# Heads normed and rotated by groups of product columns inside the tile loop

## What is computed

```python
def rms_norm(x, g):
    y = xf * lax.rsqrt(jnp.mean(xf * xf, axis=-1, keepdims=True) + EPS)
    return (y * g).astype(x.dtype)

def partial_rope(x, cos, sin):
    x1, x2, rest = xf[..., :half], xf[..., half:ROT_DIM], xf[..., ROT_DIM:]
    return jnp.concatenate([x1 * cos - x2 * sin, x2 * cos + x1 * sin, rest], axis=-1)

def qk_prep(t, g, cos, sin):
    return partial_rope(rms_norm(t, g), cos, sin)
...
hn = rms_norm(h, norm_mix[layer])
q, k, v = jnp.split(h @ w_in, ODD_SPLITS, axis=-1)
q = qk_prep(q.reshape(B, S, SWA_Q_HEADS, HEAD_DIM), qn, cos, sin)
k = qk_prep(k.reshape(B, S, SWA_KV_HEADS, HEAD_DIM), kn, cos, sin)
```

## Time and profile before

| | us |
|---|---|
| median of 3 runs | 2880.73 (2880.12 to 2882.5) |
| the profiled execution | 2879.53 |
| its span, first to last instruction | 2877.8 |
| TensorE busy | 2601.2 (90%) |
| VectorE busy | 1753.1 (61%) |
| ScalarE busy | 1206.5 (42%) |
| GpSimd busy | 632.8 (22%) |
| mean granted TensorE clock | 0.953 of 2.4 GHz |
| "qk" matmuls, first to last start | 392.5 to 655.9 |
| "all" matmuls, first to last start | 1597.6 to 1849.0 |

### The profile page before, as it was taken

One profiled execution on the slowest core, in us unless ns is written; L12 is line 12 of the kernel. 1 busy time (PEld: TensorE's weight loads), 2 busy tenths in 40 slices (PEclk: granted clock), 3 DMA queues, 4 the chain that ended last, 5 costly groups with the idle time before them and its releaser, 6 DMA issues. The chain is left out here.

```text
span 2877.8 us, 50000 instructions
## 1 busy us (share of the span) xinstructions
PE 2601.2 (90%) x14981; PEld 2201.3 (76%) x14984; DVE 1753.1 (61%) x3200; ACT 1206.5 (42%) x2278; POOL 632.8 (22%) x800
## 2 busy tenths in 40 slices
PE   6999989996979967999996899699979986999997
PEld 5999978885858866888885787578858875888786
DVE  4222245555767658776774777678843338777875
ACT  3222121114871114666764322188831114666764
POOL 3100003221110002333332233311100002434443
PEclk9999999998989978999998899899989987999999
DMA  7232223334446625776884455342235423988995
GB/s 278 99 106 105 86 87 119 102 114 160 152 146 236 233 92 210 292 290 246 303 336 186 173 173 179 118 155 88 69 112 204 175 88 131 309 292 255 343 317 133
DMA packets 171817, 524.61 MB, mean 182 GB/s; under 512 B 50232, under 2 KB 78016, under 8 KB 142656
## 3 DMA queue, kind: packets, MB, share of 16 engines
q1 hardware_dynamic: 138688, 441.27, 42.7%
q0 software_dynamic: 33024, 82.04, 9.9%
HBM read 399.14 MB, written 157.61 MB: 193 GB/s over the span
## 5 line engine op out<-in xcount | busy, mean ns | idle before, releaser
L1850 PE MATMUL ps<-moe_parts,moe_xT 128*128 (+1 forms) x2232 | 541.3, 399 | 14.0 <-issue 13.9
L1850 PEld LDWEIGHTS ps<-moe_parts,moe_xT 128*128 128x128 f32 x2232 | 417.4, 190 | 102.7 <-issue 16.3
L1989 DVE TENSOR_TENSOR moe_parts<-expert_w,moe_parts 128x1024 fp32r<-128x1024 f32 x384 | 449.8, 1219 | 33.5 <-ACT moe_parts L1930 27.0
L643 PE MATMUL ps<-in_gate_w,in_gate_hnT 128*128 128x384 f32 (+1 forms) x1536 | 318.4, 366 | 7.8 <-POOLq L614 7.8
L643 PEld LDWEIGHTS ps<-in_gate_w,in_gate_hnT 128*128 128x128 f32 x1536 | 277.9, 189 | 37.7 <-issue 7.8
L1255 PE MATMUL ps<-out_w,out_catT 128*128 128x512 f32 x1260 | 295.2, 393 | 2.5 <-ACT out_catT L1308 2.4
L1930 ACT ACTIVATE moe_parts<-expert_w 128x1024 fp32r<-128x1024 f32 x256 | 263.3, 1056 | 69.0 <-issue 46.5
L1850 PE MATMUL ps<-moe_parts,moe_hidT 128*128 (+1 forms) x1116 | 281.0, 401 | 2.6 <-ACT out_w L1951 2.6
L1255 PEld LDWEIGHTS ps<-out_w,out_catT 128*128 128x128 f32 x1260 | 234.4, 188 | 51.7 <-issue 3.2
L643 PE MATMUL ps<-in_qk_w,in_qk_hnT 128*128 128x512 f32 x1152 | 263.8, 392 | 10.1 <-DMA in_qk_hnT<-hnT_d 10.1
L643 PEld LDWEIGHTS ps<-in_qk_w,in_qk_hnT 128*128 128x128 f32 x1152 | 217.9, 189 | 55.7 <-issue 10.2
(11 more groups left out here) (257 smaller groups left out, 4051.8 us busy)
## 6 DMA issues: line engine op xcount, KB each, us to landing
expert_w<-in_w_gate SPq DMA_DIRECT2D x64, 1024.0 KB, 8.5
expert_w<-in_w_up SPq DMA_DIRECT2D x64, 1024.0 KB, 10.9
expert_w<-in_w_down SPq DMA_DIRECT2D x64, 1024.0 KB, 6.4
hnT_d<-in_gate_hnT SPq DMA_DIRECT2D x16, 1024.0 KB, 6.0
in_qk_hnT<-hnT_d SPq DMA_DIRECT2D x16, 1024.0 KB, 6.4
hn_d<-out_hn SPq DMA_DIRECT2D x32, 512.0 KB, 2.6
out_w<-y_d SPq DMA_DIRECT2D x32, 512.0 KB, 6.1
in_gate_xt<-in_x SPq DMA_DIRECT2D x16, 512.0 KB, 4.2
```

What stands on the lines that cost most here:

```text
L643: last = nc.tensor.matmul(bank(gi), hnT[:, s.slot(2), a, k, :], w[:, b, k, c0:c0 + wd], start=(a + b + k == 0), stop=((a, b) == terms_of[- ...
L1850: last = nc.tensor.matmul(out, left[:, a, k, :], right(b, k), start=(a + b + k == 0), stop=(a == 1 and k == K_ - 1))
L1989: nc.vector.tensor_tensor(parts[:, j, 1, at], K.expert_w[:, j, at], parts[:, j, 0, at].bitcast(F32), ALU.subtract).then_inc(done, 1)
```

## The change

In `project_in`, q and k heads of every tile are now squared, normed and rotated group by group, in the loop. `square_heads(s, part)` waits only for the group's own copy; `rms_heads` and `norm_rotate` run once per group, with counts `s.n * G + part + 1`. VectorE's step becomes: squares(s-1, group 2), rest(s-1, group 1), norm(s+1), rest(s-1, group 2), squares(s, 0), turn_out(s+1), rest(s, 0), squares(s, 1), add_terms(s+2). GpSimd's: `rms_tile(s+1)`, then the heads of (s-1, 2), (s, 0), (s, 1). `roped` still comes after the last group of a tile. The same elements are computed, in three times as many instructions. Behind the loop, only group 2's squares and the rests of groups 1 and 2 of the last tile are left.

```diff
--- before.py
+++ after.py
@@ -592,7 +592,7 @@
                 rms(own_, rx[:, j:j + 1], rx[:, j:j + 1], D, rms_x)
 
             def rms_heads(s, part=0, h0=0, h1=NQK):
-                alone(g, sum_q, s.n + part + 1, K.tick)
+                alone(g, sum_q, s.n * G + part + 1, K.tick)
                 rms(own_, rq[:, h0:h1], ssq[:, h0:h1], HD, rms_q)
 
             def step(s):
@@ -603,8 +603,11 @@
                 if gating:
                     alone(g, sum_v, s.n + 1, K.tick)
                     rms(own_, rv[:, :], ssv[:, :], SGU, rms_v)
-                elif not isinstance(s.n, int) or s.n >= 1:
-                    rms_heads(s.plus(-1))
+                else:
+                    if not isinstance(s.n, int) or s.n >= 1:
+                        rms_heads(s.plus(-1), G - 1, *by_group[G - 1])
+                    for part in range(G - 1):
+                        rms_heads(s, part, *by_group[part])
             rms_tile(Step(0, 0, 2))
             if gating:
 
@@ -612,10 +615,9 @@
                 own_.link(g.affine_select(out=ws[:, :, :], in_=ws[:, :, :], compare_op=ALU.is_ge, fill=0.0,
                                           base=0, pattern=[[0, SG], [1, P]], channel_multiplier=-1))
                 g.sem_inc(power_set, 1)
-            looped(g, NT, 2, 2, step, own_, 1 if kept else 3, head=1)
+            looped(g, NT, 2, 2, step, own_, 3 if gating else G if kept else G + 2, head=1)
             if qk_too:
-                for part, (h0, h1) in enumerate(by_group):
-                    rms_heads(Step(NT // 2 - 1, 1, 2), part, h0, h1)
+                rms_heads(Step(NT // 2 - 1, 1, 2), G - 1, *by_group[G - 1])
 
         @block.tensor
         def _(pe):
@@ -708,17 +710,19 @@
                 nc.vector.tensor_tensor(hnT[:, j, 1, :, :], tp.rearrange("p (k c) -> p k c", k=DK),
                                         hnT[:, j, 0, :, :].bitcast(F32), ALU.subtract).then_inc(x_low.sem, 1)
 
-            def square_heads(s, groups_out=G, h0=0, h1=NQK):
-                until(v_, act_out, s.n * G + groups_out)
+            def square_heads(s, part):
+                h0, h1 = by_group[part]
+                until(v_, act_out, s.n * G + part + 1)
                 at = slice(h0 * HD, h1 * HD)
                 qk = qk_[:, s.slot(nb), at]
                 own_.link(nc.vector.tensor_tensor(sq[:, at], qk, qk, ALU.mult))
                 nc.vector.tensor_reduce(ssq[:, h0:h1], sq[:, at].rearrange("p (h c) -> p h c", c=HD), AX, ALU.add).then_inc(sum_q.sem, 1)
 
-            def norm_rotate(s, part=0, h0=0, h1=NQK, last=True):
+            def norm_rotate(s, part):
+                h0, h1 = by_group[part]
                 n = h1 - h0
                 heads = qk_[:, s.slot(nb), h0 * HD:h1 * HD].rearrange("p (h c) -> p h c", c=HD)
-                until(v_, rms_q, s.n + part + 1)
+                until(v_, rms_q, s.n * G + part + 1)
                 own_.link(nc.vector.tensor_tensor(heads, heads, rq[:, h0:h1].unsqueeze(2).broadcast_to([P, n, HD]), ALU.mult))
                 parts = [(i, lo, hi) for i, lo, hi in ((0, h0, min(h1, NQ)), (1, max(h0, NQ), h1)) if lo < hi]
                 for i, lo, hi in parts:
@@ -738,7 +742,7 @@
                 own_.link(nc.vector.tensor_tensor(rot[:, 3, 0:n, :], x1, sin, ALU.mult))
                 own_.mark(nc.vector.tensor_tensor(x1, rot[:, 0, 0:n, :], rot[:, 1, 0:n, :], ALU.subtract))
                 own_.link(nc.vector.tensor_tensor(x2, rot[:, 2, 0:n, :], rot[:, 3, 0:n, :], ALU.add))
-                if last:
+                if part == G - 1:
                     v_.sem_inc(roped.sem, 1)
 
             def v_norm(s):
@@ -760,17 +764,23 @@
             def step(s):
                 heads_too = qk_too and (not isinstance(s.n, int) or s.n >= 1)
                 if heads_too:
-                    square_heads(s.plus(-1))
+                    square_heads(s.plus(-1), G - 1)
+                    norm_rotate(s.plus(-1), G - 2)
                 if s.plus(1).within(NT) and not (gating and isinstance(s.n, int) and s.n == 0):
                     norm(s.plus(1))
                 if gating:
                     v_norm(s)
                 if heads_too:
-                    norm_rotate(s.plus(-1))
+                    norm_rotate(s.plus(-1), G - 1)
+                if qk_too:
+                    square_heads(s, 0)
                 if s.plus(1).within(NT):
                     turn_out(s.plus(1))
                 if gating:
                     gate(s)
+                if qk_too:
+                    norm_rotate(s, 0)
+                    square_heads(s, 1)
                 if not even and s.plus(2).within(NT):
                     add_terms(s.plus(2))
             def rest(n):
@@ -806,21 +816,12 @@
             if gating:
                 v_.wait_ge(par_in, 16 * params)
                 v_.wait_ge(table_stored, 16)
-            looped(v_, NT, 2, 2, step, own_, 2 if gating else 10 if even else 11, head=1)
+            looped(v_, NT, 2, 2, step, own_, 2 if gating else 28, head=1)
             if qk_too:
-
                 end = Step(NT // 2 - 1, 1, 2)
-
-                def squares(part):
-                    square_heads(end, part + 1, *by_group[part])
-
-                def rest_of(part):
-                    norm_rotate(end, part, *by_group[part], part == G - 1)
-                squares(0)
-                for part in range(1, G):
-                    squares(part)
-                    rest_of(part - 1)
-                rest_of(G - 1)
+                square_heads(end, G - 1)
+                norm_rotate(end, G - 2)
+                norm_rotate(end, G - 1)
```

## The result

The changed kernel takes 2891.84 us in the median of 6 runs (2889.47 to 2896.98), the kernel before beside it 2880.43 (6 runs, 2878.49 to 2883.19): ratio 1.0041, 95% interval 1.0031 to 1.0051, so +9 to +15 us. It is slower, as forecast, and inside the range; it was forecast 10 us slower still. The profiled execution took 2892.36 us, its span is 2890.6 us at a mean granted clock of 0.953, the same as before.

A forecast was written before the change was run, and what follows sets the result against it. It took TensorE to bound q/k and a VectorE/GpSimd cycle of 16.02 us to bound "all". Terms +0.3 + 21.8 + 3.4 - 3.9 = +21.6 us gave 2902.3 against a median of 2880.7, range 2887 to 2914.

The forecast's parts named there:

- q/k loop: q/k stretch: VectorE's period by groups, 15.5 us, stays under TensorE's 16.32, so the change there is 0.
- the end of q/k: Behind the q/k loop: less of the last tile is left, a gain of 3.9 us (3 to 4.5).
- the end of "all": From turn_out(15) to the last rotation: 26.5 us against 23.1, +3.4 (2 to 4.5), with waits for GpSimd.
- turn_out(2): Start of the counted periods in "all": keeps its place, about +0.3 us, since TensorE's turn(2) sets it.
- The signs named beforehand: In "all": turn_out 17.7 us apart, VectorE over 80% busy, TensorE idle at transposes, powers of 1.6 and about 2.5 us.
- the period: "All" loop: 17.7 us per tile against 16.02, from 14.8 of VectorE work plus waits of 1.2, 1.05 and 0.65.
- the power of group 2 begins inside norm and stands until its end: "All" loop: GpSimd's short power held until 15.45, done at 16.0, so rest(s, 2) waits 0.65 us.
- the sum of +21.6: Whole kernel: +0.3 + 21.8 + 3.4 - 3.9 us, on the profiled execution of 2879.5.
- GpSimd finds its gaps: Rival (8%): GpSimd never stands behind VectorE in the loop; period 16.3, sum +3.4 us, 2884 us.
- Faster: Rival (4%): the x_low wait of 1.0 us per tile goes, 13 us in the loop; 2867 us.
- q/k bound by VectorE: Rival (4%): waits 1.5 us longer than reckoned use up q/k's 0.8 us to spare; 10 more, 2912 us.
- VectorE stands behind powers: Rival (4%): squares(s, 2) waits for a GpSimd power in "all"; period 18.45, 2912 us.

The follow-up runs named there:

- all_only: Kernel before with the groups in the loop only in the "all" part, q/k as before: 2898.39 us, ratio 1.0067 to the kernel before.
- short_power: Changed kernel with GpSimd taking the power of one head per group in "all"; only the stretch is read: period 15.78 us.
- sq1_first: Changed kernel with squares(s, 1) moved ahead of rest(s, 0) in "all": 2870.4 us, ratio 0.9972 to the kernel before.
- sp_early: Kernel before, no groups; in "all" add_terms(s+2) before norm_rotate(s-1), SyncE's sum store and term loads (s+4) earlier: 2862.22 us, ratio 0.9941.

## Why the prediction was right, and where it was off

**The sign and its cause: right.** The prediction said that the pace of "all" is a cycle of VectorE and GpSimd, and that groups would fill it with work and waits. `all_only` puts the whole loss in that stretch. `short_power` and `sq1_first` each bring the period back under 16 without touching TensorE, one by shorter answers, the other by cover for them.

**Terms that held.** q/k loop 0; the end of q/k -3.8 for -3.9, the last rotation 6.8 us behind ScalarE's last copy for 6.7; the end of "all" +3.2 for +3.4, with waits of 1.73 and 2.24 for 1.8 and 2.3; turn_out(2) +0.1 for +0.3. The signs named beforehand are there: TensorE's idle time at the transposes, VectorE over 80% busy, powers of 1.64 and 2.51 us.

**The term that was off: the period, 17.22 for 17.7.** Of its three waits, 1.2 came as 1.12, 1.05 as 1.00, and the 0.65 before rest(s, 2) didn't come. The step "the power of group 2 begins inside norm and stands until its end" fails in the loop: `norm` begins 0.22 us behind the rest (1723.97), the power begins at the same time (1723.98) and takes 0.70 us. In the steps written out that gap isn't there, the power begins 0.19 us into `norm`, takes 1.64, and the wait comes as 0.59 (VectorE, then GpSimd):

```profile
1620.23 1.28 DVE L703 SCALAR_TENSOR_TENSOR out_w<-in_all_xt,in_all_rx,in_all_gain 128x1024 f32<-128x1024 f32 x1
1622.10 0.29 DVE L726 TENSOR_TENSOR in_all_qk<-in_all_qk,in_all_rq 128x128 f32<-128x128 f32 x1 [0.59 <-POOL in_all_rq L583]
```

```profile
1620.42 1.64 POOL L583 TENSOR_TENSOR in_all_rq<-in_all_rq,in_all_power 128x2 f32<-128x2 f32 x1 [0.18 <-POOL in_all_rq L582]
```

VectorE's work went the other way: 17.22 less 2.12 of waits is 15.1, for 14.8. The gaps of 0.22 and 0.25 us in which it waits for its own last instruction (1723.97, 1726.79) are in the 15.1; the prediction had put nothing for the first. Together that is 0.48 x 13 = 6.2 us of the 7.1 by which the traces' +14.5 falls short of the sum of +21.6; the ends and the start make the rest.

**The rivals.** "GpSimd finds its gaps" held at one place only: the power of group 2 came in at the start of `norm`, and both instructions of group 1 stood behind `add_terms` (0.99 and 2.51 us). Its remark that without the waits `norm` becomes the late one is what `short_power` shows (0.39). "Faster" fell, by the 2.1 us of waits per tile, and its price was too high: `sq1_first` meets its condition with a period of 15.89, but that gives 1.8 us over 13 tiles and not the 13 us that the rival put on the loop. Those need a period of TensorE's own, as in `sp_early`. "q/k bound by VectorE" fell with less room than reckoned, 0.65 us for 0.8. "VectorE stands behind powers" fell: in `sq1_first` rest(s, 0) runs from 1722.66 to 1725.16, the usual 2.5 us, with the power of group 1 begun at 1723.58 and going until 1725.56. The trace thus goes against the second half of what the Trainium skill says (SBUF — State Buffer, SBUF: two separate sides and Who interferes with whom), that whichever instruction issues first holds the shared pair to its end: `add_terms` began at 1725.16, inside that power, and took its plain 1.22. In the traces read here only GpSimd was held.

**Open.** From the end of "all" (+14.5) to the end of the experts (+12.7) 1.8 us come back in the trace, in a part that the change doesn't touch; TensorE's idle time there that the profile puts down to no other engine is 9.6 us for 13.9. The measured medians are +11.4 on one occasion and +15.2 on the other, so this is within what one occasion differs from the next, and no run here tells more.

## What to carry to other kernels

Splitting a VectorE step into groups pays where TensorE's work covers VectorE and only the last tile stands open (q/k), and costs where a VectorE and GpSimd cycle is the pace, unless each answer of GpSimd has independent VectorE work ahead of it: here the order of two steps decided between +15 and -9 us. Even then the cycle itself went only from 16.02 to 15.89. Before a step is moved ahead in such a cycle, follow what it reads back through the queue that loads it; moved alone it cost 37 us, moved with its loads it gained 17. In such a sum count both sides: the waits that go (here 1.7 us a tile) and the work of the added instructions (2.9).

## What the runs showed of the hardware that was not expected

- A GpSimd power that begins at the same moment as a two-input VectorE instruction isn't held (0.70 us for 2 heads); one that begins 0.19 us into it is (1.64 us, at 1620.42), and one that begins 0.34 us into it too (1.50 us, `sq1_first`: `norm` at 1731.06, the power at 1731.40). A gap of 0.22 us on VectorE decided over 0.59 us of waiting.
- What stands on GpSimd doesn't shrink with its work: the power of one head in `short_power`, 0.55 us behind `turn_out`, took 1.43 us beside `add_terms`.
